# A two-layer hybrid trunk: the second mixer rewritten (norm applied at the projections, v for two heads at once, heads in straight code, silu by tanh, output begun early)

## The reference

```python
hn = rms_norm(h, norm_mix_g[1])
proj = h @ w_in                        # here h is hn; q, k 512 wide, v, r 1024, z 16
g = log_sigmoid(z_lr @ w_gate_up + b_gate) / 16
# per head (4 heads, q and k 128 wide, v and r 256 wide):
#   attn[t, s] = sum_k q[t] k[s] exp(b[t] - b[s])   with b the running sum of g, s <= t
#   o = attn @ v + (q exp(b)) @ state ;  the state is carried between blocks
o = o * lax.rsqrt(jnp.mean(o * o, axis=-1, keepdims=True) + EPS) * g_norm
o = o * jax.nn.silu(r)
return o.reshape(B, S, D_MODEL) @ w_out
...
h = h + sqrelu_mlp(rms_norm(h, norm_mlp_g[i]), mlp_w_up[i], mlp_w_down[i])
```

## Time and profile before

| | us |
|---|---|
| median of 3 runs (1250.64 to 1251.97) | 1251.95 |
| the profiled execution | 1251.26 |
| its span, first to last instruction | 1249.5 |
| PE busy | 1209.9 |
| DVE, ACT, POOL busy | 657.6, 466.4, 39.1 |

### The profile page before, as it was taken

The page is one execution under the profiler, slowest core; times in us unless marked ns, Lnnn a source line. Parts: engine busy times, 40 slices in busy tenths (PEclk is TensorE's granted clock), DMA queues, the critical chain, the costliest instruction groups (busy, mean ns, idle before and its releaser), DMA issues.

```text
span 1249.5 us, 15464 instructions
## 1 busy us (share of the span) xinstructions
PE 1209.9 (97%) x6021; PEld 1018.7 (82%) x6021; DVE 657.6 (53%) x861; ACT 466.4 (37%) x711; POOL 39.1 (3%) x82
## 2 busy tenths in 40 slices
PE   6999999999999999999998999989999999999996
PEld 5778888888888888888768989878888888888885
DVE  5337877644344343343368887883443443433432
ACT  5336666543223133132263433422531231331321
POOL 2000000000000000000110100100000000000001
PEclk9999999999999999999989999989999999999998
DMA  9236645524223323322103213212233222233001
GB/s 272 51 87 152 145 127 152 191 79 132 96 78 99 102 101 101 101 67 84 50 6 102 67 54 113 78 56 89 81 118 101 99 84 95 93 101 101 34 0 67
DMA packets 117867, 118.92 MB, mean 95 GB/s; under 512 B 38641, under 2 KB 87953, under 8 KB 117826
## 3 DMA queue, kind: packets, MB, share of 16 engines
q1 hardware_dynamic: 115040, 116.47, 30.7%
q10 hardware_dynamic: 2786, 1.89, 0.5%
HBM read 103.60 MB, written 2.10 MB: 85 GB/s over the span
## 4 chain that ended last, share of the span: by engine, by line
PE 89%; DVE 6%; issue 2%; ACT 2%; ACTq 0%; POOL 0%; SPq 0%; DMA 0%; DVEq 0%; POOLq 0%
PE bank L767 14%; PE bank L771 14%; PE bank L770 14%; PE bank L754 11%; PE bank L758 10%; PE bank L757 10%; PE bank L916 2%; PE bank L920 2%; PE bank L919 2%; PE bank L964 2%; DVE silu L1367 1%; PE bank L951 1%; PE bank L1051 1%; PE bank L933 1%; PE bank L934 1%
## 5 line engine op out<-in xcount | busy, mean ns | idle before, releaser
L1126 DVE TENSOR_TENSOR w_lo<-w_stage,w_hi 128x2048 fp32r<-128x2048 f32 x91 | 208.3, 2290 | 209.5 <-ACT w_hi L519 209.3
L519 ACT ACTIVATE w_hi<-w_stage 128x2048 fp32r<-128x2048 f32 x91 | 173.9, 1913 | 278.2 <-PE bank L767 224.2
L754 PE MATMUL bank<-hT_lo,w_hi 128*128 128x512 f32 x576 | 226.0, 392 | 0.0
L758 PE MATMUL bank<-hT_hi,w_lo 128*128 128x512 f32 x576 | 224.9, 390 | 0.0
L757 PE MATMUL bank<-hT_hi,w_hi 128*128 128x512 f32 x576 | 224.9, 390 | 0.0
L771 PE MATMUL bank<-w_hi,u_lo 128*128 128x512 f32 x512 | 199.2, 389 | 0.0
L767 PE MATMUL bank<-w_lo,u_hi 128*128 128x512 f32 x512 | 199.2, 389 | 0.0
L770 PE MATMUL bank<-w_hi,u_hi 128*128 128x512 f32 x512 | 199.2, 389 | 0.0
L754 PEld LDWEIGHTS bank<-hT_lo,w_hi 128*128 128x128 f32 x576 | 108.5, 188 | 23.9 <-issue 0.8
L758 PEld LDWEIGHTS bank<-hT_hi,w_lo 128*128 128x128 f32 x576 | 108.5, 188 | 22.8
L757 PEld LDWEIGHTS bank<-hT_hi,w_hi 128*128 128x128 f32 x576 | 108.4, 188 | 22.3
(11 more groups left out here) (188 smaller groups left out, 1462.1 us busy)
## 6 DMA issues: line engine op xcount, KB each, us to landing
w_stage<-in_mlp_w_up_dram SPq DMA_DIRECT2D x32, 1024.0 KB, 5.2
w_stage<-in_mlp_w_down_dram SPq DMA_DIRECT2D x32, 1024.0 KB, 4.9
w_stage<-in_fox_w_in_dram SPq DMA_DIRECT2D x32, 256.0 KB, 3.8
w_stage<-in_gla_w_in_dram SPq DMA_DIRECT2D x8, 1024.0 KB, 5.1
w_stage<-in_fox_w_in_dram SPq DMA_DIRECT2D x4, 1024.0 KB, 7.9
qa<-qk_hi SPq DMA_DIRECT2D x32, 128.0 KB
w_stage<-in_fox_w_out_dram SPq DMA_DIRECT2D x4, 1024.0 KB, 5.1
w_stage<-in_gla_w_in_dram SPq DMA_DIRECT2D x8, 512.0 KB, 3.6
```

The lines of the kernel that those rows point to most:

```text
L519: act.activation(w_hi[:, slot, :], w_stage[:, slot, :], ACT.Copy).then_inc(w_hi_made, 1)
L754: a = pe.matmul(out, w[0][:, k, :], x[1][:, k, :], start=(k == 0), stop=False)
L758: a = pe.matmul(out, w[1][:, k, :], x[0][:, k, :], start=False, stop=(k == KT - 1))
L1126: dve.tensor_tensor(w_lo[:, slot, :], w_stage[:, slot, :], fp(w_hi[:, slot, :]), ALU.subtract).then_inc(w_lo_made, 1)
```

## The change

- **Norm.** Layer 1's mixer norm no longer scales the residual. `late_norm(2, ...)`, `turn_left` and `turn_right` turn the raw residual while the last MLP group still runs, as before each MLP. GpSimd makes 1/rms for all tokens (`gla_norm`); four small matmuls with a matrix of ones spread it over the partitions (`rstd_wide`), and it is multiplied in where q, k and z leave PSUM (`keep_qk` and `z_scaled`, both on DVE), or given as a scale of ACT where v and r leave it.
- **z and the forget gate.** `gate_tile` has high and low weights side by side (48 columns), 16 matmuls in place of 24, in both layers.
- **Units.** q and k of a head share one unit; v of two heads is projected at once, with 512 columns. The stage has 12 units in place of 16.
- **Heads in straight code.** There is no hardware loop; projections of the next head stand among the levels of this one, on all engines in an order written out by hand.
- **silu.** ACT makes tanh(r/2), DVE one product for each half; the factor 1/2 and 1/rms go into `orstd` on GpSimd. The gain g_norm moves to the split of the turned output.
- **Output.** Six of the eight turns of the output (`turn_go`) and their part of the output projection (`out_early`) stand inside the last head.
- **Masks** are built ahead of the last group of MLP 0. One DMA for g_norm is issued at the start of the program, by ACT.

```diff
...
+GQK_U = (GLA_U, GLA_U + 4, GLA_U + 6, GLA_U + 9)
+GV_U = ((GLA_U + 1, GLA_U + 2), (GLA_U + 7, GLA_U + 8))
+GR_U = (GLA_U + 3, GLA_U + 5, GLA_U + 10, GLA_U + 11)
+OUT_EARLY = 6
...
+            for c in range(GLA_U, GLA_OUT_U):
+                if c in GQK_U:
+                    a, to = GQK_U.index(c), cols(w_stage, slot_of(c), 2 * DK)
+                    load(0, 0, c, to[:, :, 0:DK], gla_in_d[:, :, a * DK:(a + 1) * DK])
+                    sp.dma_start(to[:, :, DK:2 * DK], gla_in_d[:, :, GLA_K + a * DK:GLA_K + (a + 1) * DK]).then_inc(
+                        w_loaded[slot_of(c)], 16)
+                elif c in GR_U:
+                    first = 2 * GLA_K + D + RANK + GR_U.index(c) * DV
+                    load(0, 0, c, cols(w_stage, slot_of(c), DV), gla_in_d[:, :, first:first + DV])
+                else:
+                    pair = 0 if c in GV_U[0] else 1
+                    load(0, 0, c, *rows_of(gla_in_d, GV_U[pair].index(c) * (KT // 2), 2 * GLA_K + pair * S, slot_of(c)))
...
+            def gla_norm():
+                pool.wait_ge(squared, 5 * TB)
+                step(pool.tensor_tensor(ss[:, 0, :], ss[:, 0, :], ss[:, 1, :], ALU.add))
+                step(pool.tensor_tensor(ss[:, 0, :], ss[:, 0, :], mean_eps[:], ALU.add))
+                step(pool.tensor_tensor(rstd[:], ss[:, 0, :], minus_half[:], ALU.pow))
+                pool.tensor_tensor(only[:], ident[:].unsqueeze(1).to_broadcast([P, TB, P]),
+                                   rstd[:].unsqueeze(2).to_broadcast([P, TB, P]), ALU.mult).then_inc(only_made, 1)
+                pool.tensor_tensor(half_rstd, rstd[:], one_half[:], ALU.mult).then_inc(grstd_made, 1)
...
+            act.dma_start(gn, gla_norm_g.rearrange("a (j p) -> (a p) j", p=P),
+                          allow_slow_non_contiguous=True).then_inc(gn_loaded, 16)
...
+            def keep_v(pair, t):
+                act.wait_ge(gv_done, pair * TB + t + 1)
+                act.wait_ge(grstd_made, 1)
+                if pair:
+                    act.wait_ge(go_done, 4)
+                act.activation(gv[:, t, :], bank[4 + (t if pair == 0 else t % 2)][:], ACT.Copy,
+                               scale=rstd[:, t:t + 1]).then_inc(gv_copied, 1)
...
+            def tanhs(a):
+                act.wait_ge(grstd_made, 1)
+                if a % 2:
+                    act.wait_ge(go_made, a * TB)
+                for t in range(TB):
+                    act.wait_ge(r_done, a * 2 + t // 2 + 1)
+                    act.activation(silu_of(a)[:, t, :], bank[4 + t // 2][:, t % 2 * DV:(t % 2 + 1) * DV], ACT.Tanh,
+                                   scale=half_rstd[:, t:t + 1]).then_inc(tanh_made, 1)
...
+            def keep_goT(k):
+                if k == 0:
+                    act.wait_ge(gn_loaded, 16)
+                act.wait_ge(go_turned, k + 1)
+                act.activation(hT_hi[:, k, :], bank[goT_bank(k)][:], ACT.Copy,
+                               scale=gn[:, k % 2:k % 2 + 1]).then_inc(goT_hi_made, 1)
...
+            c = GLA_U
+            keep_v(0, 0)
+            keep_v(0, 1)
+            decays(0, 1)
+            exps_since(0)
+            tail_decay(0)
+            keep_v(0, 2)
+            decays(0, 2)
+            keep_v(0, 3)
+            split_hi(0, 0, c + 4)
+            decays(0, 3)
+            decays(0, 4)
+            turn_tail(0)
+            split_hi(0, 0, c + 5)
+            decays(0, 5)
+            decays(0, 6)
+            split_hi(0, 0, c + 6)
+            decays(0, 7)
+            tanhs(0)
+            squares(0)
...
+            def gate_tile(b, which, before):
+                def hi_and_lo(k):
+                    return pe.matmul(bank[b][0:GATE_ROWS, :], gates_split[:, k, which * RANK:which * RANK + GATE_ROWS],
+                                     hT_hi[:, k, :], start=(k == 0), stop=(k == KT - 1))
+                def hi_only(k):
+                    pe.matmul(bank[b][0:RANK, :], gates_split[:, k, which * RANK:(which + 1) * RANK], hT_lo[:, k, :],
+                              start=False, stop=False)
+                before(0)
+                hi_and_lo(0)
+                for k in range(1, KT):
+                    before(k)
+                    hi_only(k - 1)
+                    if k < KT - 1:
+                        hi_and_lo(k)
+                hi_only(KT - 1)
+                a = hi_and_lo(KT - 1)
+                return a
             def unit(i, per, c, shape=None, first=0):
...
+                if layer == 0:
+                    group(GROUPS - 1, None, lambda: turn_left(GLA_ADDS, False))
...
+            def project_gv(pair, t, kg):
+                c, b = GV_U[pair][kg], 4 + (t if pair == 0 else t % 2)
...
+            def turn_go(k):
+                if k < OUT_EARLY:
+                    if k < 2:
+                        pe.wait_ge(gk_copied, GLA_H)
+                        pe.wait_ge(go_made, 3 * TB)
+                    else:
+                        pe.wait_ge(goT_lo_made, k - 1)
+                else:
+                    pe.wait_ge(go_made, GLA_H * TB)
+                    pe.wait_ge(level_kept, GLA_H * (LEVELS + 1))
                 for t in range(TB):
-                    mm = pe.transpose(bank[(k + 4) % 8][:, t * P:(t + 1) * P], o_all[:, t, k * P:(k + 1) * P], ident[:])
+                    mm = pe.transpose(bank[goT_bank(k)][:, t * P:(t + 1) * P], o_all[:, t, k * P:(k + 1) * P], ident[:])
                 mm.then_inc(go_turned, 1)
+            def out_early(kg, t):
+                ks = (range(4), range(4, OUT_EARLY))[kg]
+                split_of(0, 0, GLA_OUT_U + kg)
+                pe.wait_ge(goT_lo_made, ks[-1] + 1)
+                if kg == 0 and t < 2:
+                    pe.wait_ge(silu_made, 2 * GLA_H)
+                elif kg == 0:
+                    pe.wait_ge(goT_lo_made, OUT_EARLY)
...
+            project_gqk(0, 0, range(KT), ready_late(2, GLA_ADDS, False))
+            project_gqk(0, 1, range(KT))
+            pe.wait_ge(gla_filled, 2)
+            pe.wait_ge(only_made, 1)
+            for t in range(TB):
+                mm = pe.matmul(bank[2][:, t * P:(t + 1) * P], root[:], only[:, t, :], start=True, stop=True)
+            mm.then_inc(wide_done, 1)
+            gate_tile(3, 1, lambda k: None).then_inc(z_done, 1)
+            pe.wait_ge(gup_loaded, 48)
+            pe.wait_ge(z_scaled, 1)
+            for a in range(GLA_H):
+                pe.matmul(bank[4 + a][:], gup[:, a * DK:(a + 1) * DK], zT[:], start=True, stop=True).then_inc(gate_done, 1)
+            for t in range(2):
+                project_gv(0, t, 0)
+                project_gv(0, t, 1)
+            level(0, 0)
+            project_gv(0, 2, 0)
+            project_gv(0, 2, 1)
+            level(0, 1)
+            project_gv(0, 3, 0)
+            project_gv(0, 3, 1)
+            level(0, 2)
+            project_gr(0, 0)
+            level(0, 3)
+            project_gr(0, 1)
+            turn_tail(0)
+            level(0, 4)
+            project_gr(0, 2)
+            level(0, 5)
+            outer(0)
+            project_gr(0, 3)
+            project_gqk(1, 0, lo)
+            level(0, 6)
+            project_gqk(1, 0, hi)
+            project_gqk(1, 1, lo)
+            level(0, 7)
+            project_gqk(1, 1, hi)
+            attend(0)
+            project_gr(1, 0)
+            level(1, 0)
...
+            project_gr(3, 3)
+            turn_go(0)
+            turn_go(1)
+            level(3, 3)
+            turn_go(2)
+            turn_go(3)
+            turn_tail(3)
+            level(3, 4)
+            turn_go(4)
+            turn_go(5)
+            level(3, 5)
+            outer(3)
+            out_early(0, 0)
+            level(3, 6)
+            out_early(0, 1)
+            level(3, 7)
+            out_early(0, 2)
+            attend(3)
+            out_early(0, 3)
+            for t in range(TB):
+                out_early(1, t)
+            turn_go(6)
+            turn_go(7)
             add_rows(0, 0, GLA_OUT_U, hT, lambda kg: pe.wait_ge(goT_lo_made, 4 * kg + 4), False,
-                     lambda: turn_left(1, MLP1_ADDS, False))
-            turn_right(1, MLP1_ADDS, False)
+                     lambda: turn_left(MLP1_ADDS, False), OUT_EARLY)
+            turn_right(3, MLP1_ADDS, False)
             mlp(1, MLP1_U, MLP1_ADDS)
 
 
@@ -1138,7 +1434,7 @@
                                   ALU.subtract).then_inc(w_lo_made if half else w_lo_half, 1)
...
+            def make_masks():
+                dve.wait_ge(xor_filled, 2)
+                dve.tensor_tensor(xor[:], xor[:], other[:], ALU.bitwise_xor).then_inc(xor_made, 1)
+                dve.wait_ge(xor_cut, 1)
+                for lv in range(1, LEVELS + 1):
+                    half = P >> lv
...
+            mine.then(dve.tensor_copy(fg[:, 0, :], bank[4][0:FOX_H, :]))
+            dve.tensor_tensor(fg[:, 1, :], bank[4][LO_ROW:GATE_ROWS, :], fg[:, 0, :], ALU.add).then_inc(f_summed, 1)
...
+            def keep_qk(a):
+                first = QK_BANK[0] if a == 0 else QK_BANK[1]
```

(56 more changed lines are left out.)

807 lines of the change are left out of this document (489 added, 318 removed).

## The result

The changed kernel took 1238.9 us (median of four runs, 1236.2 to 1240.4), the kernel before 1252.0 us in the runs beside them; the ratio is 0.9898 with a 95% interval of 0.9883 to 0.9913. The forecast was 1235 us with 1225 to 1244: the time lies inside, 4 us above the point. On the two profiled executions the gain is 10.8 us, where the working said 16.3, so its terms were some 5.5 us too kind. The profiled execution of after is its slowest (1240.42 us); the medians lie 13.0 us apart.

The account below looks back on a forecast made before the run. TensorE, 97% busy, was taken as the bound, losing 26.7 us in the gla stage. 26.7 + 4.9 - 14.4 - 1.8 = 15.4, + 1.8 (layer 0) - 0.9 (start) = 16.3 us off 1251.26: 1235 us, range 1225 to 1244.

Parts of the forecast that it names:

- Lost before: 26.7 us: Gla stage of the kernel before: 226.3 us long against 199.6 of full-clock work, so 26.7 us lost to waits and clock.
- New waits: 14.4 us: PE waits expected in the new stage: gates 1.0, levels 2.3, 2.2 and 2.4, head 3 4.8, last two turns 1.7 us.
- head 3: Output turn pairs wait for ACT and DVE, pushing levels 4 to 6 back: six waits plus the first r, 4.8 us.
- Clock: 1.8 us: Low granted clock in the new stage: only the stretch at 638 us stays, 1.8 us; bounds 0 and 1.8 + 3 x 2.
- a fall behind waits of 2.3 us: Rival: the clock falls in each wait of the stage, 6 us more, 1241 us; chance 0.2.
- The rival of dissolving waits: Rival: DVE and ACT reach splits earlier; three level waits and half of head 3's go, 9 us, 1226; chance 0.17.
- Work: 4.9 us less: PE work in the stage: v 3.9 us and z 1.8 less, spreading 1/rms 0.8 more; net 4.9 us less.
- the 3.9 us for the projections: Projection of v: 16 blocks of 2.96 us become 8 of 5.44, 47.4 to 43.5, a gain of 3.9 us.
- Start and layer 0: + 0.9 us: Outside the stage: layer 0's z gains 1.8 us, the extra DMA issue on ACT at the start costs 0.9.
- no change: Rival: level chain at 0.6 us each, or start and clock losses, eat the gain; chance 0.02.
- Wide v that brings nothing: Rival: a 512-column matmul of v takes as long as two of 256, losing 3.9 us, 1239; chance 0.05.
- The level chain is outrun: Rival: PE waits at all 28 levels; 0.6 us each cancels the gain, 0.9 gives 1260 us; chance 0.04.

Follow-up runs that it names:

- after again: The changed kernel itself, unaltered, timed once more beside other kernels on the same chip: 1239.3 us, ratio 0.9898 to the kernel before.
- the mend: Changed kernel with a level's decays (ACT) and decayed (DVE) ahead of the unit's split at three places: 1229.4 us, ratio 0.9827 to the kernel before.
- before + tanh: Kernel before with only silu changed, to tanh and one product per half, 1/2 folded into the gain: 1241.9 us, ratio 0.9929.
- the second experiment: Changed kernel with each 512-column block of v made as two halves of 256 columns, tokens loaded anew for each: 1241.5 us.
- the output late: Changed kernel with six output turns and eight early output rows behind attend of head 3, r's tiles spread over the levels: 1248.6 us.
- both mends: Changed kernel with decays ahead of the splits and g_norm's DMA issued behind the last MLP group: 1227.7 us, ratio 0.9819 to before.

## Why the prediction was right, and where its terms were off

**Lost before: 26.7 us.** Measured 16.2 us idle + 8.2 of low clock on work, 24.4. The other 2.3 us are of the size of what the twelve waits of before hide, some 0.2 us each. Of the idle time, 2.8 us stood in head 0 and not at the two ends where the prediction looked.

**New waits: 14.4 us.** Measured 12.6. The three chains counted from a PE event stand where they were forecast: 2.31, 2.28 and 2.41 us against 2.3, 2.2 and 2.4. The gates' wait was 0.87 against 1.0, the last turns' 1.88 against 1.7. Off was head 3: 2.7 us in five waits, not 4.8 in six. My walk let each pair of turns push back the levels behind it in full. A level's own chain can run on while a pair waits, so that the two waits overlap; that is how I read it, and no run tested it.

**Clock: 1.8 us.** This step failed in the profiled execution. It was 5.1 us, and none of it at 638 us, where I had put it. I took a rival's effect (a fall behind waits of 2.3 us) for unlikely because the gaps of before were 2.8 us or longer. The trace of after has a low stretch behind two of its three such waits (670.62 and 772.44 us, not 682.54) and behind the 1.88 us. Of the rival's 6 us more, 3.3 came in this execution, and in after again 4.9 (6.7 us, half of it at 640 us). In others less came: the four executions of after have mean clocks of 0.993 (the profiled one), 0.993, 0.995 and 0.996, and 0.003 of the span is 3.7 us, which leaves an estimated 1.4 us for the stage in the fastest. So 1.8 us is one end of what this term does, and no single number holds for it. The rival of dissolving waits is refuted by the three idles and by the mend that removes them.

**Work: 4.9 us less.** Measured 3.0, and with what waits hide this is good to some 1.5 us: before and before + tanh run the same matmuls, and their rests are 234.7 and 233.1 us (249.1 - 9.5 idle - 6.5). The step that failed in every execution, and the largest miss, is the 3.9 us for the projections. Summed from start to start, with idle time and low clock taken out, the matmuls of 256 and 512 columns take 171.6 us before and 171.2 after: 0.5 us less. The width itself brought 2.5 us. The hand-overs from fp32 work (levels, turns, outer products, attends) to an fp32r projection took 2.0 back. At 256 columns they fell from 2.5 to 1.4 us, since there are 16 blocks in place of 32. At 512 columns they rose from 0.7 to 3.8 us, since the order after cuts these matmuls into 25 stretches, where before had 5. I had priced the old blocks by a row that has a hand-over in its 2.96 us, and the new ones by a row without one. In the other direction, the gates took 3.1 us instead of 3.6 (though the first matmul behind them takes 0.64 us in place of 0.35, counted above), and outer products, attends, turns and levels together 0.9 us less, in part ends of waits. z and the spreading of 1/rms came as forecast (24 matmuls to 16, and 0.81 us). That the hand-over costs this is read from rows of three kernels; no run took it away by itself.

**Start and layer 0: + 0.9 us.** Measured 1.0, by luck of two errors. The extra DMA cost 1.8 us at the first square instead of 0.9, since I priced its issue and not what it does to a later one; and a wait of 1.14 us for a DMA in the attention (at 88.96 us in before) dissolved.

The sum: 24.4 - 12.6 - 5.1 + 3.0 = 9.7 us in the stage, + 1.0 ahead of it, 10.8 us with what rounding drops. Against the forecast's 16.3 the lost time is 2.3 us too high, the clock 3.3 and the work 1.9, and only the waits, 1.8, go the other way. The range held these errors; the point stood on chains that were right and on two prices that were not. Of the other rivals, no change falls by the 13.0 us. Wide v that brings nothing falls by the second experiment as far as the width goes, though with the hand-overs only 0.5 us of the projections' 3.9 came. The level chain is outrun in after at three places only, but the output late shows that its mechanism is near: without cover, levels 6 and 7 of head 3 wait 1.0 and 1.6 us, what follows them waits longer, and the whole gain but 2.8 us is gone.

## What to carry to other kernels

When two engines split a weight in turn (high part, then low part), put the short operations that the busiest engine waits for ahead of the split in both queues: three such swaps were worth 7.7 us of the stage here. Walk each chain from the event on the busiest engine that starts it. This gave the long waits to 0.1 us, while the projections' gain, priced from a block that holds a hand-over against one that doesn't, was 0.5 us in place of 3.9, and the clock's term 5.1 in place of 1.8. And test the cheapest part of a rework alone: the tanh on its own brought 9.4 us, where the whole brought 13.0.

## What the runs showed of the hardware

- Behind an fp32 level or turn the first fp32r matmul takes 0.31 us from start to start at 512 columns instead of 0.227, and 0.20 at 256 columns instead of 0.120; behind an outer product or attend, whose fp32 matmuls have 256 columns, 0.42 at 512. Cutting a long projection for a level costs about 0.1 us each time.
- The granted clock fell to 0.50 behind waits of 2.4 us and less, one of them the 0.87 us ahead of the gates, and not each time: the same program had its low stretches at 672, 776 and 850 us in one execution and at 640, 672 and 776 in another. The kernel with both mends had none between the MLPs, and its fastest run (1224.9 us) and slowest (1231.4) differ by a mean clock of 0.997 and 0.994.
- An issue of a DMA of 256 single numbers took 0.58 us on ACT's queue and lengthened a later issue from 1.90 to 3.17 us.
